# Two trunk layers of a hybrid encoder: the norm crossings' tokens in three parts, weight splits after the first norm step, and the first recurrent head's evictions ahead of its products

## What is computed

```python
def layer(x, p):                                   # x: 560 tokens x 1024
    h = rmsnorm(x, p['g_pre_mix'])
    (qn, qr, ckv, kr, qb, kb, vb, qc, kc, vc, alr, gc, gate) = split(h @ p['w_in'])
    oa = latent_attention(qn, qr, ckv, kr)         # branch A, rotary keys shared by 8 heads
    ob = window_attention(qb, kb, vb)              # branch B
    oc = gated_linear_attention(qc, kc, vc, alr)   # branch C, 4 heads, decay gates from alr
    g = sigmoid(gate)
    mix = (g[0]*(oa @ p['w_up_a']) + g[1]*(ob @ p['w_up_b']) + g[2]*(oc @ p['w_up_c'])) @ p['w_out']
    x = x + rmsnorm(mix, p['g_post_mix'])
    f = square(relu(rmsnorm(x, p['g_pre_mlp']) @ p['w_ff1'])) @ p['w_ff2']
    return x + rmsnorm(f, p['g_post_mlp'])
```

## Time and profile before

| | |
|---|---|
| three runs | 2378.67, 2380.45 (median), 2380.99 us |
| the profiled execution | 2381.46 us, its span 2379.7 us |
| PE busy | 2311.7 us, 97% of the span |
| DVE, ACT, POOL busy | 918.9, 1001.0, 936.5 us (39 to 42%) |
| mean granted TensorE clock | 0.993 |
| chain that ended last | PE 90%, DVE 6%, ACT 2% |

### The profile page before, as it was taken

One profiled execution on the slowest core, in us unless ns is written; L12 is line 12 of the kernel. 1 busy time (PEld: TensorE's weight loads), 2 busy tenths in 40 slices (PEclk: granted clock), 3 DMA queues, 4 the chain that ended last, 5 costly groups with the idle time before them and its releaser, 6 DMA issues.

```text
span 2379.7 us, 41755 instructions
## 1 busy us (share of the span) xinstructions
PE 2311.7 (97%) x17728; PEld 2187.3 (92%) x17728; DVE 918.9 (39%) x1861; ACT 1001.0 (42%) x1895; POOL 936.5 (39%) x598
## 2 busy tenths in 40 slices
PE   7999999999999899999989999999999998999997
PEld 7899978889899899999979999788899998999997
DVE  5556455543514401001555664555344153000014
ACT  5344334433555552332344443343336555423322
POOL 2222224344665354544412222144445643645432
PEclk9999999999999999999999999999999999999999
DMA  5122221112224122222321222211222241222222
GB/s 191 49 64 60 90 66 56 52 55 79 63 81 155 54 89 83 87 89 64 123 70 52 71 67 81 67 54 54 68 66 63 86 166 39 86 89 82 88 76 79
DMA packets 59369, 187.73 MB, mean 79 GB/s; under 512 B 8048, under 2 KB 17104, under 8 KB 58672
## 3 DMA queue, kind: packets, MB, share of 16 engines
q1 hardware_dynamic: 49680, 165.62, 22.2%
q10 hardware_dynamic: 9504, 19.44, 2.6%
HBM read 170.87 MB, written 10.89 MB: 76 GB/s over the span
## 4 chain that ended last, share of the span: by engine, by line
PE 90%; DVE 6%; ACT 2%; issue 1%; POOL 1%; DMA 0%; ACTq 0%; SPq 0%; DVEq 0%; POOLq 0%
PE dense L862 42%; PE att L862 29%; PE att L937 2%; PE att L1150 2%; PE att L1076 1%; PE att L1013 1%; PE att L1096 1%; PE att L1188 1%; PE att L1017 1%; PE att L999 1%; PE dense L891 1%; PE att L1121 1%; PE att L1223 1%; DVE h_raw L1820 1%; PE att L1101 1%
## 5 line engine op out<-in xcount | busy, mean ns | idle before, releaser
L2192 POOL TENSOR_TENSOR wlo<-wraw,whi 128x1024 fp32r<-128x1024 f32 x245 | 588.6, 2410 | 609.1 <-ACT whi L1275 609.1
L862 PE MATMUL dense<-h_hi,whi 128*128 128x280 f32 x1888 | 559.1, 296 | 12.1 <-DVE cproj L1710 5.1
L862 PE MATMUL dense<-h_lo,whi 128*128 128x280 f32 x1888 | 552.1, 292 | 0.0
L862 PE MATMUL dense<-h_hi,wlo 128*128 128x280 f32 x1888 | 551.0, 292 | 0.0
L1275 ACT ACTIVATE whi<-wraw 128x1024 fp32r<-128x1024 f32 x302 | 314.9, 1051 | 291.2 <-DMA wraw<-in_w 266.9
L862 PEld LDWEIGHTS dense<-h_hi,whi 128*128 128x128 f32 x1888 | 356.7, 189 | 25.7 <-issue 13.0
L862 PEld LDWEIGHTS dense<-h_hi,wlo 128*128 128x128 f32 x1888 | 356.2, 189 | 0.6
L862 PEld LDWEIGHTS dense<-h_lo,whi 128*128 128x128 f32 x1888 | 356.6, 189 | 0.0
L862 PE MATMUL att<-h_hi,whi 128*128 128x280 f32 x1024 | 301.4, 294 | 11.8 <-ACT whi L1275 11.8
L862 PE MATMUL att<-h_lo,whi 128*128 128x280 f32 x1024 | 300.0, 293 | 0.0
L862 PE MATMUL att<-h_hi,wlo 128*128 128x280 f32 x1024 | 299.6, 293 | 0.0
(11 more groups left out here) (353 smaller groups left out, 4632.8 us busy)
## 6 DMA issues: line engine op xcount, KB each, us to landing
wraw<-in_w SPq DMA_DIRECT2D x302, 512.0 KB, 3.6
x_spill<-x ACTq DMA_DIRECT2D x2, 2240.0 KB, 7.3
x<-x_spill ACTq DMA_DIRECT2D x2, 2240.0 KB, 12.1
k_cat<-k_rope ACTq DMA_DIRECT2D x16, 212.0 KB, 3.5
x<-in_x SPq DMA_DIRECT2D x4, 560.0 KB, 6.0
out_y_out<-x SPq DMA_DIRECT2D x4, 560.0 KB, 3.1
out_c_out<-ckv SPq DMA_DIRECT2D x2, 560.0 KB, 5.4
state<-in_state ACTq DMA_DIRECT2D x8, 128.0 KB, 2.1
```

Of the source, the lines that this page charges most:

```text
L862: mm = pe.matmul(bank(u, o, hf)[0:m, :], a[:, k, o * 128:o * 128 + m], b[:, k, H[hf]], start=(k == 0 and i == 0), stop=(k == kt - 1 and i ...
L2192: pool.tensor_tensor(wlo[slot][:, :], wraw[slot][:, :], whi[slot][:, :].bitcast(F32), ALU.subtract).then_inc(pool_done, st.done("pool", f" ...
```

## The change

1. `tokens` is a step in three parts (tiles 0 to 3, 4 and 5, 6 and 7). At a crossing's half 0 the last half unit's eviction comes behind the first part, and a new step `last sum` adds its square behind the second.
2. At a crossing's half 1, a `free` step stands behind the first of the four norm steps, so two splits go there; the square of `x` is now a step of its own, behind them. The third split moves to the `free` behind the pair's evictions, ahead of the last norm step.
3. Head 0 of branch C: `v arg 0`, `v arg 1` move behind the eviction of `ck0` and the split of `cg0`; `v lev 0` moves behind the evictions of `cv0`, `cv1`, `ckv0`; `v lev 1`, `v end`, `v lev 2` behind `ckv1` and two splits. PE waits for `gla lev {h} 3` in `p lev 1`.
4. The 8 copies of `k_rope` are issued by SP, behind the loads of `gate_c0` and `up_c0`, and no longer by ACT; one split moves behind `prep_a` 3.

```diff
             def lap(l, post, pre, first, second):
...
+                def crossed(hf, j):
+                    plan.extend([(l, ("norm", post, hf, j)), (l, ("square", pre, hf, j))])
+
+                def begun(hf, parts):
+                    plan.extend([(l, ("tokens", pre, hf, p)) for p in parts])
...
+                    if i == LAP - 2 and pre:
+                        plan.append((l, ("ms", pre, 0)))
+                        begun(0, (0,))
+                if not pre:
+                    return
+                begun(0, (1,))
+                plan.append((l, ("last sum",)))
+                begun(0, (2,))
+                plan.extend([(l, ("rstd", post, 1)), (l, ("norm", post, 1, 0)), (l, ("free",)), (l, ("square", pre, 1, 0))])
+                crossed(1, 1)
+                plan.append((l1, ("pair", units[0:2], 0, (l, post))))
+                crossed(1, 2)
+                plan.extend([(l1, ("after", v, 0)) for v in units[0:2]] + [(l, ("free",))])
+                crossed(1, 3)
+                for i, u in enumerate(units[2:], 2):
...
-                gla_steps((0, "p z"), (0, "v decay"), (0, "v arg 0"), (0, "v arg 1"))
+                gla_steps((0, "p z"), (0, "v decay"))
                 for u in V_NEXT[2:]:
                     order.append(("half", u, 1))
                     if UNITS[u] == ("ck", 0):
-                        gla_steps((0, "v lev 0"), (0, "v arg 2"))
-                    if UNITS[u] == ("cv", 0):
-                        gla_steps((0, "v lev 1"), (0, "v end"))
-                    if u == V_NEXT[-1]:
-                        gla_steps((0, "v lev 2"))
+                        gla_steps((0, "v arg 0"), (0, "v arg 1"))
+                gla_steps((0, "v lev 0"), (0, "v arg 2"))
                 dense()
                 order.append(("prep_a", "square"))
+                gla_steps((0, "v lev 1"), (0, "v end"), (0, "v lev 2"))
                 dense()
...
-                        order.extend([("dense", u, "late"), ("prep_a", 3), ("evac", u, None)])
+                        order.extend([("dense", u, "late"), ("prep_a", 3), ("evac", u, None), ("free",)])
...
+            PARTS = (range(0, 4), range(4, 6), range(6, KD))
...
+                def spread_keys(l, first):
+                    if first == 0:
+                        sp.wait_ge(dve_done, A("dve", "rope k", l))
+                        sp.wait_ge(a_loaded["a_kr"], 32 * (l + 1))
+                    else:
+                        sp.wait_ge(dve_done, A("dve", "qrot 1", l))
+                        sp.wait_ge(act_done, A("act", "qraw 1", l))
+                    for h in range(first, first + 4):
+                        sp.dma_start(k_cat[64:128, h, :], k_rope[64:128, :]).then_inc(k_spread, 16)
...
                         one = level_of(1)
+                        pe.wait_ge(dve_done, A("dve", f"gla lev {h} 3"))
...
+                    elif step[0] == "last sum":
+                        add_waiting()
```

More of the change, by code:

```diff
@@ new lines, in crossed @@
+                def crossed(hf, j):
+                    plan.extend([(l, ("norm", post, hf, j)), (l, ("square", pre, hf, j))])
+                def begun(hf, parts):
+                    plan.extend([(l, ("tokens", pre, hf, p)) for p in parts])
+                (l0, ends), (l1, units) = first, second
+                plan.append((l, ("rstd", post, 0)))
+                crossed(0, 0)
+                crossed(0, 1)
+                for i, u in enumerate(ends):
+                    if i in (1, 2):
+                        crossed(0, i + 1)
+                    if i == LAP - 3 and pre:
+                        plan.append((l, ("hold",)))
+                    if i == LAP - 2 and pre:
+                        plan.extend([(l, ("sums", pre, 0)), (l, ("rstd", pre, 0))])
+                    plan.append((l0, ("half", u, 1)))
+                    if i == 0:
+                        plan.append((l, ("ms", post, 0)))
+                    if i == LAP - 2 and pre:
+                        plan.append((l, ("ms", pre, 0)))
+                        begun(0, (0,))
@@ L645, in program @@
                     crossing = True
-                if step[0] == "tokens" and step[2] == 1:
+                if step[0] == "tokens" and step[2:] == (1, 2):
                     crossing = False
@@ L654, in program @@
                     begun = True
-                most = {"half": 0 if step[1:] and step[1] in U_B else 1, "dense": 2, "splits": 1, "free": 2, "pair": 0}[step[0]]
+                most = {"half": 0 if step[1:] and step[1] in U_B else 1, "dense": 2 if len(step) == 2 else 0, "splits": 1, "free": 2, "pair": 0}[step[0]]
                 if held:
@@ L1592, in _ @@
                         w_hi(step[1])
+                    elif step[0] == "square" and len(step) == 4:
+                        square_of(*step[1:])
                     elif step[0] == "square":
@@ L1812, in lo @@
                             st.mark("dve", f"{which} lo {m} {hf}")
-                    for k in range(KD):
+                    for k in PARTS[part]:
                         g = g_pre_mix[:, (l + 1) * KD + k:(l + 1) * KD + k + 1] if which == "next" else p_("g_" + which, k)
@@ L2158, in _ @@
                     elif step[0] == "tokens":
-                        tokens(step[1], step[2])
+                        tokens(*step[1:])
                     elif step[0] == "gla":
```

85 lines of the change are left out of this document (32 added, 53 removed).

## The result

| | before | after |
|---|---|---|
| median of 4 runs, us | 2380.4 (2378.7 to 2381.0) | 2359.5 (2359.1 to 2360.8) |
| profiled execution: time, span, mean clock | 2381.5, 2379.7, 0.993 | 2359.1, 2357.3, 0.994 |
| ratio of the medians, 95% interval | | 0.9913 (0.9900 to 0.9926) |

A forecast was written before the change was run, and what follows sets the result against it. TensorE was taken to bound the kernel, so only its waits counted. Head 0's 12.4, 5.3 before the MLPs, 1.2 into layer 1 and 0 at the keys made 18.9 us off 2381.5: 2362.5 us, range 2357 to 2370.

The forecast's parts named there:

- Head 0: Head 0 of both layers: PE's waits for evictions vanish with their aftermath, 4.9 and 7.5 us, together 12.4 (8 to 13).
- rival 1: Head 0: POOL goes twice for each DVE product, ckv1 comes late, 5 to 6 us back, 2368 us; 12%.
- "wrong if" sign: Head 0: a DVE product held for over 1.2 us twice in a row would show the forecast wrong.
- Crossings before the MLP: Both crossings before an MLP: second mean square earlier, less clock loss; 2.6 us each, 5.3 together (1.0 to 3.7 each).
- the clock's: Crossings before an MLP: 1.2 GHz after PE's wait costs 2.0 us, part of it in gaps, about 0.8 remaining.
- Crossing into layer 1: Crossing into layer 1: second mean square 2.6 us earlier, 1.4 off for the clock, leaving 1.2 (0 to 2.7).
- Rotary keys: Rotary keys: copies moved to SP and one split earlier give 0 us (-0.5 to +1).
- 2 (waits paid in full): Crossings: three moved waits each cost 2.8 us of 1.2 GHz with no gap, 5 us back, 2367.5 us; 13%.
- 3: Head 0: DVE's evictions still wait because whi of cg0 finds its weights late; only 6.5 us remain, 2375 us; 3%.
- 4: Rotary keys: SP blocked by the rotation beyond the 17 us between load and whi, loads late, slower, 2386 us; 2%.

The follow-up runs named there:

- experiment 2: Two runs on the changed kernel: head 0's exponentials back at their old place, 2364.2 us; head 0's products back between the evictions, 2364.9 us.
- experiment 5: Two runs on the changed kernel: key copies back on ScalarE, earlier split kept, 2358.0 us; copies left on SyncE, that split four evictions later, 2357.8 us.
- the last kernel but one of experiment 7: The first of experiment 7 plus the fourth norm step and its square ahead of the pair's second eviction at the crossings: 2348.9 us.
- the last one: The last kernel but one of experiment 7 plus half 1's first four tokens ahead of the second eviction after the root: 2347.3 us.
- the first of experiment 7: Changed kernel with all three splits behind the first norm step, key copies on ScalarE, and the root one eviction earlier at each crossing: 2350.5 us.

## Why the prediction was right, step by step

- **Head 0**: 12.4 forecast, 12.6 by the traces (4.96 and 7.68), 14.1 when undone. Right. The reason I gave, that DVE stands 7.75 us for the late split and the evictions come late behind it, is only half of it in layer 0: with that stand still there, but no products ahead of the evictions, PE did not wait (experiment 2). In layer 1 both moves are needed. `whi` of `cg0` came at 47.99 (47.2 forecast), `wlo` at 49.79 (49.2), `ckv1` at 60.95 (61.1). The path there was other than I had it: in layer 0 not four products held 0.6 us each, but one held 2.4 and three free; in layer 1 they took 0.52, 0.87, 0.87 and 1.26 us, nearer to my sum. That one was passed by more than one operation of POOL: rival 1's mechanism did occur, for one product of four, and cost nothing. The "wrong if" sign, two in a row held for over 1.2 us, did not appear.
- **Crossings before the MLP**: 2.6 each forecast, 3.2 and 3.3 measured. The chain was right: the first mean square 1.0 earlier (1.1 forecast), the two 19.0 apart (19), a wait of 4.15 (4.2), PE idle 6.06 (6.4), one such wait in place of the two for `whi`. The term that was mis-sized is the clock's. It fell (0.82 and 0.79 over 12 us), and I charged 0.8 net of the gaps; of the 3.4 us at the tokens only 0.2 was lost.
- **Crossing into layer 1**: 1.2 forecast, 2.2 measured. I had the mean square 2.6 us earlier and took 1.4 off for the clock. It came 2.8 earlier, and the clock did fall (0.88); it took 1.0 at once, but 0.4 of that lay in a gap at the tokens that PE had before, so 0.6 was lost. Again the clock's term was mis-sized, and the result was in the upper part of the bounds.
- **Rotary keys**: 0 forecast (bounds -0.5 and 1), 1.8 measured, outside them. The step that failed: "its 2 us hold on DVE falls on another operation of the same chain: 0". It did fall on the same chain, but a hold's length depends on where in POOL's 2.4 us the operation starts: in layer 0 a hold of 2.0 us became one of 1.5, in layer 1 one of 2.2 became 1.6, and one of 0.7, on the first product of the keys, fell away. Moving the copies was not free either: with the earlier split, it is what puts the hold back, 1.5 us (experiment 5). The earlier split with the copies left on ScalarE takes away all 3.3 us of that wait; the copies on SyncE with no split moved was not run.
- **Not in the sum**: the kernel's start, 0.8 us longer after, with no step of the change there: the first matmuls start 0.23 us apart until 18.7 us before and until 20.4 us after, and 0.13 apart from there on, so the part at 1.2 GHz lasts longer in that execution. That is chance.
- **Rivals**: 2 (waits paid in full) didn't come: the clock fell at all three crossings, as it says, but the price lay in gaps. 3 and 4 are out: the evictions don't wait, and PE waits for no load; the block of SP's queue lies well within the 17 us. The errors add up: 0.2 + 1.2 + 1.0 + 1.8 - 0.8 = 3.4, of the 3.5 between the sum's 18.9 and the traces' 22.4. By the medians the gain is 20.9, 2.0 over the sum; the third us between 2362.5 and 2359.5 is that I took the sum off the profiled execution (2381.5) and not off the median (2380.4). All terms but the start's erred to the same side, so the total held by its wide range more than by its parts.

## What to carry to other kernels

When two engines pass work to each other through in-order queues, price each step where it stands in the queue and not by its own length: a split of 1.2 us cost 4 of waiting because ScalarE's half stood behind two evictions, and moving it ahead of them gave 7 us for no change in the work. After each such gain look at what is late next; here that was in turn a split, a square, and a token, each one eviction too late, while a root moved ahead of an eviction only put that eviction ahead of the tokens. And before moving DMA issues off a queue, ask what they were holding back: here they kept a weight split out of VectorE's way.

## What the runs showed of the hardware

- The clock after a wait is not set by the wait's length alone. In the crossing into layer 1, a wait of 2.22 us was followed by 0.86 in the last kernel but one of experiment 7 (the first two rows below), and the same wait by 1.00 in the last one (the third row, and the second of the stretches above). Within one kernel, the first of experiment 7, a wait of 2.82 us before layer 0's MLP was followed by 0.86 over 12 us, and one of 2.81 before layer 1's by 1.00. My prediction had weighed waits of 3.2 and 3.4 us by their lengths. The Trainium skill ("TensorE: Matmul & The Clock Gate", What's actually happening) has it that recent activity decides, on a count that runs freely; both pairs agree.

```profile
1191.92 0.74 PE L938 MATMUL att<-nsum,const 128*128 128x280 f32 x2 [2.22 <-DVE nsum L1804]
```

```profile
1190.00:1202.00 12.00, 10.08 (x64) 9.99 (x65) 8.66 (x19) 6.33 (x13) 0.00 (x0) 0.86 0.23 97
```

```profile
1192.04 0.74 PE L940 MATMUL att<-nsum,const 128*128 128x280 f32 x2 [2.22 <-DVE nsum L1806]
```

- VectorE and GpSimd did not always take turns: in the changed kernel's layer 0 a VectorE product of 0.45 us, both inputs in SBUF, took 2.83 us (57.11 to 59.94), while GpSimd began two operations of 0.65 and 0.66 us (57.35, 57.96) and the group behind them (58.57), and the next product took 0.45. In layer 1 the same four products took 0.52, 0.87, 0.87 and 1.26 us, each held by less than 0.9 us.
